# Column-form up blocks on one Trainium2 core: matmuls ordered by width over a whole chunk, the gate's closing chunk pair by pair

## The reference

```python
f = jnp.square(jax.nn.relu(h @ w_ff1[l])) @ w_ff2[l]          # first block, width 4096

def _swiglu(x, wg, wu, wd):                                    # four times, width 2816
    return (jax.nn.silu(x @ wg) * (x @ wu)) @ wd
```

## Time and profile before

| What | Value |
|---|---|
| Median of three runs | 1384.62 us (1384.59 to 1384.69) |
| Profiled execution, its own time | 1384.48 us |
| Its span, first to last instruction | 1382.7 us |
| TensorE busy | 1370.2 us, 99% of the span |
| VectorE busy | 890.4 us, 64% |
| ScalarE busy | 742.0 us, 54% |
| Share of PE in the chain that ended last | 98%, of it 20% on line 1654 and 10% on line 1657 |

### The profile page before, as it was taken

One profiled execution on the slowest core, in us unless ns is written; L12 is line 12 of the kernel. 1 busy time (PEld: TensorE's weight loads), 2 busy tenths in 40 slices (PEclk: granted clock), 3 DMA queues, 4 the chain that ended last, 5 costly groups with the idle time before them and its releaser, 6 DMA issues.

```text
span 1382.7 us, 18120 instructions
## 1 busy us (share of the span) xinstructions
PE 1370.2 (99%) x7261; PEld 1158.4 (84%) x7261; DVE 890.4 (64%) x1037; ACT 742.0 (54%) x984; POOL 150.8 (11%) x251
## 2 busy tenths in 40 slices
PE   8999999999999999999999999999999999999998
PEld 7988888888888888877788888888888877788886
DVE  5986657656567666665876566666666646676663
ACT  6647555444455444465765444554444667554443
POOL 1000101111011111110211110021170100000000
PEclk9999999999999999999999999999999999999999
DMA  9953345756648556554357666585655644365550
GB/s 295 311 183 130 133 164 163 241 189 203 201 139 265 188 190 199 179 189 139 127 168 230 194 201 199 168 238 191 193 192 169 204 147 137 117 233 185 194 170 31
DMA packets 121363, 255.38 MB, mean 185 GB/s; under 512 B 6394, under 2 KB 32830, under 8 KB 121279
## 3 DMA queue, kind: packets, MB, share of 16 engines
q1 hardware_dynamic: 117036, 250.99, 55.5%
q0 software_dynamic: 4096, 3.15, 0.9%
q10 hardware_dynamic: 146, 0.07, 0.0%
HBM read 253.14 MB, written 1.05 MB: 184 GB/s over the span
## 4 chain that ended last, share of the span: by engine, by line
PE 98%; ACT 1%; DVE 0%; issue 0%; DMA 0%; POOL 0%; DVEq 0%; ACTq 0%; POOLq 0%
PE ps L1654 20%; PE ps L1364 18%; PE ps L1366 18%; PE ps L1365 18%; PE ps L1657 10%; PE ps L1352 1%; PE ps L1354 1%; PE ps L1353 1%; PE ps L1387 1%; PE ps L1377 1%; PE ps L1424 1%; PE ps L1469 1%; PE ps L1631 1%; PE ps L1397 1%; PE ps L1692 1%; PE ps L1451 0%
## 5 line engine op out<-in xcount | busy, mean ns | idle before, releaser
L972 DVE TENSOR_TENSOR w_lo<-raw,w_hi 128x2048 fp32r<-128x2048 f32 x225 | 516.8, 2301 | 275.2 <-ACT w_hi L679 273.9
L679 ACT CAST w_hi<-raw 128x2048 fp32r<-128x2048 f32 x225 | 428.2, 1910 | 210.0 <-PE ps L1366 136.5
L1654 PE MATMUL ps<-hT,w_hi 128*128 128x512 f32 x1216 | 304.4, 392 | 0.1
L1654 PEld LDWEIGHTS ps<-hT,w_hi 128*128 128x128 f32 x1216 | 220.0, 189 | 40.5 <-issue 0.3
L1364 PE MATMUL ps<-w_hi,yT_hi 128*128 128x512 f32 x640 | 252.9, 395 | 0.7 <-DVE yT_lo L1232 0.7
L1366 PE MATMUL ps<-w_hi,yT_lo 128*128 128x512 f32 x640 | 249.5, 390 | 0.0
L1365 PE MATMUL ps<-w_lo,yT_hi 128*128 128x512 f32 x640 | 249.4, 390 | 0.0
L1364 PE MATMUL ps<-w_hi,hT 128*128 128x512 f32 (+1 forms) x496 | 193.8, 391 | 0.0
L1366 PE MATMUL ps<-w_hi,hT 128*128 128x512 f32 (+1 forms) x496 | 188.6, 380 | 0.0
L1365 PE MATMUL ps<-w_lo,hT 128*128 128x512 f32 (+1 forms) x496 | 188.2, 379 | 0.0
L1657 PEld LDWEIGHTS ps<-hT,w_lo 128*128 128x128 f32 x1216 | 165.9, 190 | 11.9
(11 more groups left out here) (196 smaller groups left out, 1256.9 us busy)
## 6 DMA issues: line engine op xcount, KB each, us to landing
raw<-ffn_wd SPq DMA_DIRECT2D x44, 1024.0 KB, 5.3
raw<-ffn_wg SPq DMA_DIRECT2D x40, 1024.0 KB, 6.0
raw<-ffn_wu SPq DMA_DIRECT2D x40, 1024.0 KB, 5.4
raw<-w_ff SPq DMA_DIRECT2D x32, 1024.0 KB, 5.9
raw<-diff_w_in SPq DMA_DIRECT2D x12, 1024.0 KB, 5.2
raw<-na_w_in SPq DMA_DIRECT2D x12, 1024.0 KB, 5.2
raw<-w_in SPq DMA_DIRECT2D x10, 1024.0 KB, 6.4
raw<-w_xkv SPq DMA_DIRECT2D x8, 1024.0 KB, 11.3
```

Source lines behind the costliest of these rows:

```text
L679: act.copy(hi_part(c), raw[:, c % NRAW, :]).then_inc(hi_done, 1)
L972: dve.tensor_tensor(lo_part(c), raw[:, c % NRAW, :], hi_part(c), ALU.subtract).then_inc(lo_done, 1)
L1654: pe.matmul(ps[:, 4 + j, :], wh[:, i, j * P:j * P + P], h_both[:, 4 * last + i, :, :], start=first and i == 0, stop=False)
```

## The change

In `by_columns` the opening chunk (`ga`, `ua`, of relu too) does both pairs' wide matmuls and then both pairs' narrow ones. The closing up chunk `ub` of a glu stage does both pairs' narrow ones and then both pairs' wide ones. The other closing chunks (`gb`, and `ub` of relu) stay pair by pair, but pair 0 goes narrow then wide, pair 1 wide then narrow; a chunk given in halves goes narrow then wide in each. The wait for a pair's banks stays at the pair's first matmul of the opening chunk.

```diff
-                for pair in halves_of(word):
-                    if first and is_up:
+                def banks_free(pair):
+                    if is_up:
                         pe.wait_ge(sum_done, sums_count(kind, b, 0, pair))
...
+                def weights(high, pair, begins, ends):
+                    if begins:
+                        banks_free(pair)
+                    for j in (2 * pair, 2 * pair + 1):
+                        for i in range(4):
+                            k, cols = 4 * last + i, slice(j * P, j * P + P)
+                            start, stop = begins and i == 0, ends and i == 3
+                            if high:
+                                ins = pe.matmul(ps[:, 4 + j, :], wh[:, i, cols], h_both[:, k, :, :], start=start, stop=stop)
+                            else:
+                                ins = pe.matmul(ps[:, 4 + j, 0:256], wl[:, i, cols], hT[0][:, k, :], start=start, stop=stop)
+                    return ins
+
+                pairs = halves_of(word)
+                if first or is_up:
+                    for pair in pairs:
+                        weights(first, pair, first, False)
+                    for pair in pairs:
+                        finish(weights(not first, pair, False, last), word, pair)
+                else:
+                    for pair in pairs:
+                        high_first = pair == 1 and word.half is None
+                        weights(high_first, pair, False, False)
+                        finish(weights(not high_first, pair, False, last), word, pair)
```

More of the change, by code:

```diff
@@ L1642, in by_columns @@
                     h_ready(word.at + 1, t, int(last))
-                for pair in halves_of(word):
-                    if first and is_up:
+                def banks_free(pair):
+                    if is_up:
                         pe.wait_ge(sum_done, sums_count(kind, b, 0, pair))
-                    elif first and b - 1 not in ROW_BLOCKS[kind]:
+                    elif b - 1 not in ROW_BLOCKS[kind]:
                         pe.wait_ge(sum_done, sums_count(kind, b - 1, 1, pair))
-                    elif first and kind != "relu" and pair == 0:
+                    elif kind != "relu" and pair == 0:
@@ L1649, in by_columns @@
                         pe.wait_ge(gate_done, TT * gates_before(kind, 0) + TT)
-                    elif first:
+                    else:
                         pe.wait_ge(hid_lo, TT * (beta - (2 if kind == "relu" and pair == 0 else 1)) + TT)
[L1652 to L1659, removed]
+                def weights(high, pair, begins, ends):
[10 more added lines that the diff above has]
+                    return ins
```

## The result

| What | Before | After |
|---|---|---|
| Median | 1384.61 us | 1391.24 us |
| Ratio, with its 95% interval | | 1.0052 [1.0042, 1.0062] |
| Profiled execution, its own time | 1384.48 us | 1391.82 us |
| Its span | 1382.7 us | 1390.1 us |
| TensorE busy | 1370.2 us | 1373.3 us |

The change makes the kernel 6.6 us slower (forecast 6.5).

What follows compares the result with a forecast made beforehand. The prediction took TensorE, 99% busy, as the bound, its time the sum of its paces. Stalls of 8.22 us less 1.76 us of pace gave +6.46 us, 1384.62 to 1391.1 us, with range 1388.9 to 1392.9.

Steps and rivals of the forecast that it cites:

- What bounds the kernel: Whole kernel: TensorE, 99% busy; an edit to its order can only change the matmuls' pace or make TensorE stand.
- Part 1, the pace: All column-form chunks: 88 fewer ways back from narrow to wide matmuls at 0.02 us each, 1.76 us less.
- Part 2, the second wait: `ua` of 16 glu blocks: pair 1's wait comes earlier than its sum, so TensorE stands, 8.22 us more.
- the price of going on: After a late sum in `ua`, TensorE's stream resumes as if started 0.17 us after the release; ends 0.06 and 0.22.
- A regular block: `ua` of blocks 2 to 4, eleven of the twelve: a stall of 0.44 us each, 4.84 us together.
- Block 1: `ua1` of block 1, four times: the sum waits for the split as well; 0.65 us each, 2.60 us together.
- Block 4 of glu2: `ua` there, where sums are late already: pair 1's sum comes after its turn, a stall of 0.78 us.
- Part 3, what costs nothing: `ub`'s later pair 0 and `Z`, earlier second waits in `ga` and relu's `ua`, opening chunks' later pair 0: no cost.
- That the pace gains nothing: Rival, whole kernel: the stalls come but fewer width changes save nothing, 1392.8 us; chance 0.07.
- the split is out of the way: Rival, blocks 2 to 4: split no longer ahead of pair 0's sum, only block 1 stalls, 1385.5 us; chance 0.06.
- TensorE works on while the sum is late: Rival, at the late sums: TensorE continues with queued matmuls and only the pace counts, 1382.9 us; chance 0.05.

Runs made afterwards that it cites:

- the split behind the sums: Changed kernel with VectorE's split moved behind both sums of Y (block 1: behind Y1.1), ScalarE's cast staying: 1380.93 us, ratio 0.9984 to the kernel before.
- `ua` by pair: Changed kernel with only the glu stages' `ua` put back to wide 8, narrow 8, wide 8, narrow 8: 1383.0 us, ratio 0.9990 to the kernel before.
- the split alone: Kernel before the change, with only VectorE's split moved behind the sums of Y: 1383.99 us, ratio 0.9999 to the kernel before.
- `ua` alone over the chunk: Kernel before the change, with only the glu stages' `ua` as wide 16, narrow 16: 1391.11 us, ratio 1.0058 to the kernel before.

## Why the prediction was right, point by point

**What bounds the kernel** held: an edit of TensorE's order costs where TensorE is made to stand, and all of that reached the end; nothing later gave it back.

**Part 1, the pace: 1.76 us less.** Right. The kernel with the split behind the sums has that order, and it loses time in block 4 of glu2 alone (0.33 us, as much as the kernel before loses there). Without its first stretch it takes 1.8 us less than before. `ua` by pair, with 72 narrow runs gone, takes 1.0 less where 1.44 was reckoned, and 0.26 of the difference is its longer stall in block 4 of glu2. The formula of the Trainium skill (TensorE: Matmul & The Clock Gate, Back-to-back issue gap) has a matmul's own width alone, and the page gives it for an isolated matmul; for this stream, in which a change of width cost about 0.02 us, it does not hold.

**Part 2, the second wait: 8.22 us more.** The mechanism, the place and the time of the sum (2.11 us after `ua`'s start) were right. The term came out about a tenth too small, by the price of going on and by block 4 of glu2. A regular block lost 0.49 by its 16 wide matmuls where 0.44 was reckoned: TensorE goes on 0.05 us after the sum, against 0.06 in the earlier trace rows, but the first 8 matmuls then take 1.98 us instead of 1.81, 0.17 and not the 0.11 that the first step alone shows. The rows used for that price went no further than the second matmul.

Block 1 is closer, here of glu0; its sum ends at 435.13 + 0.68 = 435.81 and pair 1 goes on after it. The changed kernel, and then the kernel with the split behind the sums, where nothing waits:

```profile
431.69 3.81 PE L1663 MATMUL ps<-hT,w_hi 128*128 128x512 f32 x16
435.87 2.11 PE L1663 MATMUL ps<-hT,w_hi 128*128 128x512 f32 x8 [0.37 <-DVE att_bias L1277]
437.82 4.00 PE L1665 MATMUL ps<-hT,w_lo 128*128 128x256 f32 x32
```

```profile
431.67 5.63 PE L1663 MATMUL ps<-hT,w_hi 128*128 128x512 f32 x24
437.14 1.11 PE L1665 MATMUL ps<-hT,w_lo 128*128 128x256 f32 x8
```

The 24 wide matmuls take 6.13 us in the one and 5.47 in the other: 0.66 lost, where 0.65 was reckoned. Block 4 of glu2 lost more than its 0.78, because its first wait became later too:

```profile
1026.14 1.11 PE L1665 MATMUL ps<-hT,w_lo 128*128 128x256 f32 x8
1027.62 2.08 PE L1663 MATMUL ps<-hT,w_hi 128*128 128x512 f32 x8 [0.37 <-DVE att_bias L1277]
1030.21 2.11 PE L1663 MATMUL ps<-hT,w_hi 128*128 128x512 f32 x8 [0.51 <-DVE att_bias L1277]
1032.16 1.11 PE L1665 MATMUL ps<-hT,w_lo 128*128 128x256 f32 x8
```

```profile
1023.73 3.15 DVE L972 TENSOR_TENSOR w_lo<-raw,w_hi 128x2048 fp32r<-128x2048 f32 x1 [2.81 <-ACT w_hi L679]
1026.80 0.68 DVE L1277 TENSOR_TENSOR att_bias<-ps,att_bias 128x512 f32<-128x512 f32 x1
```

Eight narrow ones and the step to `ua` take 1.48 us instead of 0.95: 0.53 lost, where 0.26 was lost before. `ua`'s 16 wide take 4.54, 0.89 too long. The split takes 3.15 us there, where it took 2.90 before (and 2.29 in the other blocks), and the prediction took the times of that block over from before as they were.

The whole of the stalls shows between two kernels with the same order on TensorE: the changed one takes 9.0 us more than the one with the split behind the sums (7.2 + 1.8 in the table above), where 8.22 were reckoned. Less the pace's 1.8 that is 7.2 us; timed within either group of executions, the changed kernel and the one before differ by 6.8 to 6.9 us (1389.8 against 1382.9, 1391.5 against 1384.7). So the forecast's 6.5 was a little low, by the stalls, and that the medians' 6.6 comes so near to it is in part luck.

**Part 3, what costs nothing**, held: `ua` by pair keeps all those moves and, but for block 4 of glu2, runs at the pace alone.

**The rivals.** That the pace gains nothing fell with the split behind the sums, 1.8 us under before where the split alone gives 0.2. That the split is out of the way did not come by itself, but made on purpose it took the stalls away as the rival said, and those of block 1 too, whose split was moved as well. Pair 1's sum then ended 1.51 us after `ua`'s start and not 1.29, and came 2.77 us after pair 0's and not the 2.58 that the prediction called fixed: its copy starts only at 499.94, 0.20 us after `ua`, when `gb` is done with the pair. That TensorE works on while the sum is late fell with the rows at 503.06.

## What to carry to other kernels

When instructions of a full engine are regrouped, look not only at what the grouping saves but at every wait that comes earlier by it: here 0.95 us of work left the place between two waits where a chain had only 0.70 to spare, and a gain of 1.8 us turned into a loss of 6.6. Read the chain behind the wait back to what really sets it; here that was a split queued ahead of the sum on VectorE, and moving it, worth next to nothing by itself (0.2 us), made the regrouping pay. The idle time printed before the matmuls, 4.2 us, was less than half of the 9.0 us lost: take the distances of the starts.

## What the runs showed of the hardware that was not expected

**The two groups.** The first product's matmuls of 256 columns, in the profiled execution of before and in that of `ua` alone over the chunk:

```profile
12.38 2.07 PE L1567 MATMUL ps<-hT,w_hi 128*128 128x256 f32 x8 [0.89 <-ACT hT L710]
14.25 1.91 PE L1572 MATMUL ps<-hT,w_hi 128*128 128x256 f32 x8
```

```profile
12.57 1.21 PE L1567 MATMUL ps<-hT,w_hi 128*128 128x256 f32 x8 [1.23 <-ACT hT L710]
13.62 1.12 PE L1572 MATMUL ps<-hT,w_hi 128*128 128x256 f32 x8
```

Eight of them take 1.87 us in the one and 1.05 in the other. Once in line they start 0.213 us apart in the one, the pace of the lower of TensorE's two levels (1.2 GHz) for 256 columns, and 0.12 us apart in the other. Before this product TensorE has done little but transposes. In the trace of before the step falls from 0.213 to 0.120 us at 16.8 us, and there the trace's record of the full granted clock begins; what the profile prints for the time ahead of it (9 in the first slice) does not show the lower level, which is read from the pace. That record begins between 16.7 and 17.3 us in eight of the ten profiled executions, and at 10.9 and 12.0 us in the other two, those that have their first column-form matmul 1.6 to 2.0 us earlier in the table above. The kernel before was profiled once, but by their times its executions fall in both groups too (1382.6 to 1383.0 and 1384.3 to 1385.0 us). The shift of some 1.7 us is about the size of part 1.

**VectorE beside POOL.** VectorE's split takes 2.29 us alone, and more in most places where POOL subtracts the bias masks (line 660) at the same time: in block 4 of glu2 it takes 2.90 us before and 3.15 after the change. The split of before, and two of POOL's subtractions, one ahead of it and one beside it:

```profile
1019.02 2.90 DVE L972 TENSOR_TENSOR w_lo<-raw,w_hi 128x2048 fp32r<-128x2048 f32 x1 [3.05 <-ACT w_hi L679]
```

```profile
1017.77 1.02 POOL L660 TENSOR_TENSOR big<-tab,big 128x384 f32<-128x384 f32 x1
...
1019.73 3.06 POOL L660 TENSOR_TENSOR big<-tab,big 128x384 f32<-128x384 f32 x1
```

POOL's subtraction takes 1.02 us alone and 3.06 beside the split. The Trainium skill, SBUF — State Buffer, section SBUF: two separate sides, has the two engines share a pair of ports that one of them holds for a whole instruction, where VectorE's has two inputs in SBUF and POOL's reads SBUF. That the split grows by less than one of POOL's instructions, and POOL's by less than one split, agrees with it, though no run here tells it from another kind of contention.
